# One start remainder modulo 512 bytes for all operands of TensorE in a decoder-block kernel

## The chip, the cores and the metric

The kernel runs on one core of one Trainium2 chip. The metric is the device time of one execution in microseconds (us), the median of a few runs.

## The reference

The reference is one hybrid decoder layer on a sequence of 1024 tokens of width 1024, in float32:

```python
x = x + 0.5 * gt1 * swiglu(mod(rmsnorm(x)), ffn1_w1, ffn1_w3, ffn1_w2)   # width 2816
x = x + gt2 * hybrid_mixer(mod(rmsnorm(x)), w_in, ..., w_out)            # below
x = x + 0.5 * gt3 * swiglu(mod(rmsnorm(x)), ffn2_w1, ffn2_w3, ffn2_w2)
return modulate(rmsnorm(x, g_final), shf, scf)
```

The shifts, scales and gates come from a conditioning vector through a matrix of 1024 x 11264. The mixer projects to q, k, v and three gates; 4 heads are causal differential attention (two softmax maps each, with rotary embedding), 8 channel groups a gated convolution over 3 tokens; both are normalised, joined and projected back.

## The kernel before

Everything is held transposed: features in the 128 partitions, tokens along a partition, in halves of 512. Each float32 operand of a large product is split into a high and a low part (names that end in h and l: `Wh`, `Wl`), and each product of 128 x 128 by 128 x 512 is three matmuls into one PSUM bank: high by high, high by low, low by high. In every one the first operand (128 columns, 512 bytes of a partition) is loaded into the array as weights, the stationary operand, and the second (512 columns, 2048 bytes) streams through it, the moving operand. `mm` (line 1532) and `mm_open` (line 1536) issue them; `nc.tensor.transpose` at lines 1970 and 1890 turns attention's tiles.

The two feed-forward blocks (0.5 * gate * SwiGLU) use one level of Strassen's scheme, 7 products in place of 8. Their stages, twice each:

- **plain group**, 192 matmuls, the first units of weights in the ordinary way (`plain_group`);
- **up**, 140 products j = 0 to 6 in turn, each of 12 matmuls (4 k steps x 3): stationary `Wh`, `Wl` (eight slots, filled by ScalarE and VectorE five products ahead), moving `Bh`/`Bl` number j, which are kept for the whole stage (`up`, matmuls at line 1536). Product 0 streams `Bh0`, and so on;
- **down**, 77 products of 12 matmuls (4 output tiles x 3): both operands are slots of `Wh` and `Wl` (`down_tile`, line 1536).

Between them lies the mixer, with matmuls from line 1532: projections with stationary `Mh`/`Ml` and moving `Hh`/`Hl` (24 matmuls a job, 8 k steps x 3), the output projection with moving `Gh`/`Gl` and others, and a stage that makes V in which `Hh`/`Hl` are stationary and `Mh`/`Ml` moving. Attention interleaves projections for the next head with small float32 matmuls, each recorded twice.

All tiles are placed by hand in a partition. `place` (lines 152 to 160) puts a tile at a given byte offset; the first free byte is 16512, which is 128 more than a multiple of 512. Two groups of places follow from it:

```python
base = at[0]                      # 16512: remainder 128 modulo 512
x_at = base + 88 * K + 64         # remainder 192; K is 1024
slot_at, raw_at, t_at, z_at, tmp_at = (x_at + n * K for n in (32, 64, 80, 96, 108))
```

At remainder 128 lie `Bh`/`Bl` 0, 1, 2, 3 and 5 (from `base`), `Mh`, the weights' sums `Sums`, `QK[:, 0]`, and `G2[:, 0]`. At remainder 192 lie `Wh`, `Wl`, `Raw`, `T`, `X`, `Ada`, the temporaries, `Bh`/`Bl` 4, 6 and `B12` (in places of X and others), and, because of the 8 spare elements in `QK`, also `O`, `Hh`, `Hl`, `Ml`, `Wo`, `V`, `Gh`, `Gl`. `QK[:, 1]` and `G2[:, 1]` lie at 160. Slices of an operand along k or along its 128 columns step by multiples of 512 bytes, so a tile's remainder is that of all its slices of 128 or 512 columns.

The order of the work is written out by hand; each engine runs its own list and waits on semaphores. SP and POOL issue the loads, the spills to DRAM and their reloads, each released by the engines' counts.

Of the kernel before, what the change touches and what calls it, by code (L numbers as in the profile page):

```python
# [6 lines left out]
F32R = mybir.dt.float32r  # L7
# [4 lines left out]
P = 128  # L12
D = 1024
S = 1024
# [136 lines left out]
def program(nc, up_w, down_w, units, ada, x_t, cols_d, lam_d, rope_d, square_d, out_t):  # L151
    ctx = ExitStack()
    with ctx:
# [3 lines left out]
        def place(name, shape, dtype=F32, like=None):  # L157

            size = 4
            for n in shape[1:]:  # L160
                size *= n
            offset = at[0] if like is None else like
            if like is None:
                at[0] += (size + 31) // 32 * 32
            return nc.alloc_sbuf_tensor_at(name, shape, dtype, offset=offset), offset

        K = 1024
        base = at[0]
        x_at = base + 88 * K + 64
        slot_at, raw_at, t_at, z_at, tmp_at = (x_at + n * K for n in (32, 64, 80, 96, 108))  # L170
        at[0] = tmp_at + 8 * K

        X, _ = place("X", [P, NH, KT, HALF], like=x_at)
# [10 lines left out]
        Sums, _ = place("Sums", [P, 4, HALF], like=base + 80 * K)  # L184
        Wh, _ = place("Wh", [P, SLOTS, HALF], F32R, like=slot_at)
        Wl, _ = place("Wl", [P, SLOTS, HALF], F32R, like=slot_at + 16 * K)
        Raw, _ = place("Raw", [P, 4, 2, HALF], like=raw_at)
        T, _ = place("T", [P, 8, HALF], like=t_at)
        Ada, _ = place("Ada", [P, 2, D], like=z_at)
        AdaSum, _ = place("AdaSum", [P, D], like=z_at + 8 * K)  # L190
        W2s, _ = place("W2s", [P, 4, HALF], like=tmp_at)
# [3 lines left out]
        RawB, _ = place("RawB", [P, 8, HALF], like=raw_at)  # L195

        AdaFirst, _ = place("AdaFirst", [P, KT, D], like=base)
        AdaSecond, _ = place("AdaSecond", [P, KT, D], like=base + 32 * K)
        AdaSum0, _ = place("AdaSum0", [P, D], like=t_at)
        AdaRow, _ = place("AdaRow", [P, D], like=t_at + 4 * K)  # L200
        Lam4, _ = place("Lam4", [P, 4, DH], like=t_at + 8 * K)
        LamP, _ = place("LamP", [P, 2, DH], like=t_at + 9 * K)


        Mh, _ = place("Mh", [P, RING, S], F32R, like=base)
        qk_at = base + 12 * K
        QK, _ = place("QK", [P, 2, S + 8], like=qk_at)
        CU, _ = place("CU", [P, S + 2], like=qk_at)
        CT, _ = place("CT", [P, S], like=qk_at + 4 * (S + 8))
        o_at = qk_at + 8 * (S + 8)  # L210
        O, _ = place("O", [P, QB, P], like=o_at)
        Mr, _ = place("Mr", [P, RING, S], like=o_at + 4 * K)
        h0_at = o_at + 16 * K
# [3 lines left out]
        Ml, _ = place("Ml", [P, RING, S], F32R, like=h0_at + 32 * K)  # L217

        Wo, _ = place("Wo", [P, 2, 2, S], F32R, like=h0_at)
        Rope, _ = place("Rope", [P, 2, S], like=h0_at + 44 * K)  # L220
        assert h0_at + 52 * K == x_at
        V, _ = place("V", [P, QB, HEADS * P], like=raw_at)
        Gh, _ = place("Gh", [P, GF, S], F32R, like=t_at)
        Gl, _ = place("Gl", [P, GF, S], F32R, like=t_at + 8 * K)
        NextQ, _ = place("NextQ", [P, S], like=t_at + 4 * K)
        NextK, _ = place("NextK", [P, S], like=t_at + 12 * K)

        G2, _ = place("G2", [P, 2, S + 8], F32R, like=qk_at)
        PR, _ = place("PR", [P, 3, S], like=z_at)
        SqSum, _ = place("SqSum", [P, NH, HALF], like=z_at)  # L230
        Sq, _ = place("Sq", [P, 2, HALF], like=z_at + 4 * K)
        Spread, _ = place("Spread", [P, NH, HALF], like=z_at + 8 * K)
        TmpA, _ = place("TmpA", [P, 2, HALF], like=tmp_at)
        TmpG, _ = place("TmpG", [P, 2, HALF], like=tmp_at + 4 * K)
        DT, _ = place("DT", [P, S], like=tmp_at + 4 * K)
        Out, _ = place("Out", [P, NH, KT, HALF], like=h0_at)

        Square, _ = place("Square", [P, 2, P])
        Cols, _ = place("Cols", [P, NCOLS])
        Mod, _ = place("Mod", [P, SECTIONS * KT])  # L240
        Scale, _ = place("Scale", [P, 4, KT])
        Gate, _ = place("Gate", [P, 3, KT])
        CAct, _ = place("CAct", [P, KT])
        Ones, _ = place("Ones", [P, 1])
        Mean, _ = place("Mean", [P, 1])
        MeanG, _ = place("MeanG", [P, 2])
        EpsC, _ = place("EpsC", [P, 2])
        Root, _ = place("Root", [P, 8])
        Inv, _ = place("Inv", [P, 8])
        LamS, _ = place("LamS", [P, 8])  # L250
        SubG, _ = place("SubG", [P, 1])
        NMax, _ = place("NMax", [P, 2])
        Sum, _ = place("Sum", [P, 2])
        RSum, _ = place("RSum", [P, QB, 2])
        Ratio, _ = place("Ratio", [P, 1])
        Junk, _ = place("Junk", [P, P])
        SqO, _ = place("SqO", [P, QB])
        assert at[0] <= nc.sbuf_usable_end

# [1826 lines left out]
```

## Time and profile before

| what | value |
|---|---|
| median of 3 runs | 1899.19 us (1899.11 to 1899.46) |
| profiled execution, its own time | 1899.21 us |
| its span, first to last instruction | 1897.4 us |
| PE (TensorE matmul) busy | 1842.2 us, 97% of the span, 8394 matmuls |
| PEld (weight loads) busy | 1476.9 us, 78% |
| VectorE (DVE) busy | 1260.6 us, 66% |
| ScalarE (ACT) busy | 774.0 us, 41% |
| GpSimd (POOL) busy | 273.6 us, 14% |
| DMA | 269.77 MB, mean 142 GB/s |

Times inside the span count from its start. Matmuls are pipelined: the next one starts before the recorded end of the last (each is shown as about 0.39 us long, and starts follow one another every 0.23 us), so the distance between starts is what a matmul costs, and the duration printed is not. The stages by the chain of waits: feed-forward 1 with its plain group to about 103 us, up to 497 us, down to 704 us; the mixer to about 1226 us; feed-forward 2 with its plain group to 1281 us, up to 1670 us, down to the end.

### The profile page before, as it was taken

The page shows a single profiled execution, that of the slowest core. Times are in us where ns is not written, and L with a number is a line of the kernel's source. Part 1 is how long each engine was busy: PE and PEld are TensorE (multiplying, and loading weights), DVE is VectorE, ACT ScalarE, POOL GpSimd, SP SyncE. Part 2 cuts the span into 40 slices and gives each one's busy share as a digit, 9 for nine tenths or more (in the row PEclk, how much of TensorE's full clock was granted, in tenths as well). Part 3 has the DMA queues.
Part 4 walks back from the last instruction along what each step waited for, and adds up shares of the span by engine and source line. Part 5 has one row for each costly group of instructions (what it writes and reads, how often), then busy time and mean ns, then how long its engine had stood idle before and what let it go on. Part 6 is the DMA issues. An engine that isn't in the chain of part 4 may idle for free.

```text
span 1897.4 us, 23217 instructions
## 1 busy us (share of the span) xinstructions
PE 1842.2 (97%) x8394; PEld 1476.9 (78%) x8394; DVE 1260.6 (66%) x1952; ACT 774.0 (41%) x1392; POOL 273.6 (14%) x411
## 2 busy tenths in 40 slices
PE   6999999999999999999999999999999999999997
PEld 3778888888788877888877777787888888878885
DVE  5887777767486776434226668787767666577767
ACT  4643333333344555111125556563333333344445
POOL 2011211211220000000303430101111111112000
PEclk9999999999999999999999999999999999999998
DMA  8165565664775312111201110325444544487432
GB/s 317 68 232 194 198 219 193 220 211 174 263 214 157 100 61 78 45 45 45 67 34 45 45 34 1 139 95 188 168 182 172 205 157 166 151 269 217 128 100 89
DMA packets 100529, 269.77 MB, mean 142 GB/s; under 512 B 13120, under 2 KB 13504, under 8 KB 100288
## 3 DMA queue, kind: packets, MB, share of 16 engines
q1 hardware_dynamic: 62608, 146.30, 22.3%
q0 software_dynamic: 34304, 117.46, 18.1%
q10 hardware_dynamic: 3504, 4.53, 1.0%
q8 instruction: 67, 1.10, 0.2%
q14 instruction: 46, 0.38, 0.1%
HBM read 209.53 MB, written 54.53 MB: 139 GB/s over the span
## 4 chain that ended last, share of the span: by engine, by line
PE 82%; DVE 8%; ACT 4%; issue 2%; DMA 1%; POOL 1%; ACTq 1%; DVEq 0%; POOLq 0%
PE PS L1536 60%; PE PS L1532 22%; ACTq L877 1%; DMA AdaFirst<-ada 1%; DMA TmpA<-TmpA 1%; DVE NMax L1447 1%; DVE X L1107 1%; PE PS L1970 1%; DVE SqSum L1312 0%; DVE Wl L1006 0%; DVE TmpA L1330 0%; DVE X L1343 0%; ACT X L676 0%; POOL TmpA L571 0%; ACT PR L899 0%
## 5 line engine op out<-in xcount | busy, mean ns | idle before, releaser
L1536 PE MATMUL PS<-Bh,Wh 128*128 128x512 f32 x1120 | 441.4, 394 | 3.8 <-ACT T L659 3.8
L1536 PE MATMUL PS<-Bl,Wh 128*128 128x512 f32 x1120 | 440.6, 393 | 0.0
L1536 PE MATMUL PS<-Bh,Wl 128*128 128x512 f32 x1120 | 439.9, 393 | 0.0
L1536 PEld LDWEIGHTS PS<-Bh,Wh 128*128 128x128 f32 x1120 | 209.7, 187 | 55.8 <-issue 3.7
L1536 PEld LDWEIGHTS PS<-Bh,Wl 128*128 128x128 f32 x1120 | 209.8, 187 | 50.1
L1536 PEld LDWEIGHTS PS<-Bl,Wh 128*128 128x128 f32 x1120 | 209.8, 187 | 48.9
L1536 PE MATMUL PS<-Wh 128*128 128x512 f32 x616 | 240.3, 390 | 3.4 <-DVE Wl L1041 1.7
L1536 PE MATMUL PS<-Wl,Wh 128*128 128x512 f32 x616 | 239.7, 389 | 0.0
L1536 PE MATMUL PS<-Wh,Wl 128*128 128x512 f32 x616 | 239.7, 389 | 0.0
L1038 DVE TENSOR_TENSOR Wl<-RawB,Wh 128x512 fp32r<-128x512 f32 x154 | 106.6, 693 | 136.4 <-ACT Wh L634 135.2
L634 ACT ACTIVATE Wh<-RawB 128x512 fp32r<-128x512 f32 x154 | 97.5, 633 | 229.9 <-PE PS L1536 229.9
L659 ACT ACTIVATE T<-PS 128x512 f32<-128x512 f32 x120 | 71.7, 598 | 257.2 <-PE PS L1536 257.2
L1006 DVE TENSOR_TENSOR Wl<-Sums,Wh 128x512 fp32r<-128x512 f32 x160 | 110.4, 690 | 89.0 <-ACT Wh L624 88.9
L1536 PEld LDWEIGHTS PS<-Wh 128*128 128x128 f32 x616 | 115.6, 188 | 28.2 <-DVE T L1072 2.5
L1006 DVE TENSOR_TENSOR Wl<-Raw,Wh 128x512 fp32r<-128x512 f32 x136 | 94.1, 696 | 62.4 <-ACT Wh L624 61.9
L1536 PEld LDWEIGHTS PS<-Wh,Wl 128*128 128x128 f32 x616 | 115.6, 188 | 24.2
L1536 PEld LDWEIGHTS PS<-Wl,Wh 128*128 128x128 f32 x616 | 115.6, 188 | 23.9
L1532 PE MATMUL PS<-Hh,Mh 128*128 128x512 f32 x320 | 131.0, 409 | 2.1 <-DVE Hl L1336 1.3
L624 ACT ACTIVATE Wh<-Sums 128x512 fp32r<-128x512 f32 x160 | 98.4, 623 | 79.6 <-DVE Sums L1024 52.5
L1532 PE MATMUL PS<-Hl,Mh 128*128 128x512 f32 x320 | 126.6, 396 | 0.0
L1532 PE MATMUL PS<-Hh,Ml 128*128 128x512 f32 x320 | 126.1, 394 | 0.0
L1062 DVE TENSOR_TENSOR T<-T,PS 128x512 f32<-128x512 f32 x120 | 82.3, 686 | 47.0 <-PE PS L1536 44.8
(195 smaller groups left out, 2894.8 us busy)
## 6 DMA issues: line engine op xcount, KB each, us to landing
Raw<-up_w SPq DMA_DIRECT2D x86, 512.0 KB, 5.1
Ada<-ada POOLq DMA_DIRECT2D x72, 512.0 KB, 4.3
g_dram<-T SPq DMA_DIRECT2D x88, 256.0 KB, 2.0
W2s<-down_w POOLq DMA_DIRECT2D x88, 256.0 KB, 4.3
s_dram<-W2s POOLq DMA_DIRECT2D x88, 256.0 KB, 2.4
GQ<-g_dram POOLq DMA_DIRECT2D x88, 256.0 KB, 3.6
RawB<-s_dram SPq DMA_DIRECT2D x88, 256.0 KB, 2.8
RawB<-down_w SPq DMA_DIRECT2D x66, 256.0 KB, 2.7
```

The lines of the kernel that those rows point to most:

```text
L624: nc.scalar.activation(Wh[:, slot, :], src, ACT.Copy).then_inc(w_hi, 1)
L634: nc.scalar.activation(Wh[:, 4 + m % 4, :], RawB[:, m % 8, :], ACT.Copy).then_inc(w_hi, 1)
L659: nc.scalar.activation(T[:, 4 * w + q, :], PS[:, x + (j == 1), :], ACT.Copy).then_inc(acopy, 1)
L877: act.dma_start(to[a:a + 32, :], TmpA[a ^ 32:(a ^ 32) + 32, slot, :]).then_inc(shifted[j % 2], 16)
L1006: nc.vector.tensor_tensor(Wl[:, slot, :], src, Wh[:, slot, :].bitcast(F32), ALU.subtract).then_inc(w_lo, 1)
L1038: nc.vector.tensor_tensor(Wl[:, 4 + m % 4, :], RawB[:, m % 8, :], Wh[:, 4 + m % 4, :].bitcast(F32), ALU.subtract).then_inc(w_lo, 1)
L1062: nc.vector.tensor_tensor(T[:, 4 * w + q, :], T[:, 4 * w + q, :], PS[:, x + (j != 4), :], ALU.add)\
L1107: nc.vector.tensor_tensor(out, left, right, ALU.subtract).then_inc(t_sum, 1)
L1447: nc.vector.tensor_reduce(NMax[:, c:c + 1], scores(c, 0, i + 1), AX.X, ALU.max, negate=True)\
L1532: return nc.tensor.matmul(out, lhs, rhs, start=first, stop=last)
L1536: return nc.tensor.matmul(out, lhs, rhs, start=first, stop=last, skip_group_check=True)
L1970: made = nc.tensor.transpose(PS[:, 4 + r, blk(b % 4)], PR[:, 2, blk(b)], ident)
```

## The change

Only places change. `x_at` moves by 960 bytes from `base + 88 * K + 64` to `base + 89 * K`, so that all tiles reckoned from it are at remainder 128. `QK` and `G2` get rows of S + 128 instead of S + 8 elements, so that their second rows, and `O` and all behind it up to X, are at remainder 128 too. `Junk`, 512 bytes that ScalarE writes and nobody reads, gets no place of its own and lies in the new spare part at the end of the second row of `QK`. No instruction, wait or DMA is added, removed or reordered.

```diff
-        x_at = base + 88 * K + 64
+        x_at = base + 89 * K
...
-        QK, _ = place("QK", [P, 2, S + 8], like=qk_at)
+        QK, _ = place("QK", [P, 2, S + P], like=qk_at)
         CU, _ = place("CU", [P, S + 2], like=qk_at)
-        CT, _ = place("CT", [P, S], like=qk_at + 4 * (S + 8))
-        o_at = qk_at + 8 * (S + 8)
+        CT, _ = place("CT", [P, S], like=qk_at + 4 * (S + P))
+        o_at = qk_at + 8 * (S + P)
...
-        G2, _ = place("G2", [P, 2, S + 8], F32R, like=qk_at)
+        G2, _ = place("G2", [P, 2, S + P], F32R, like=qk_at)
...
-        Junk, _ = place("Junk", [P, P])
+        Junk, _ = place("Junk", [P, P], like=o_at - 4 * P)
```

## Rows read from the trace of the kernel before

**Rows 1.** The page, part 1: busy time, share of the span, instructions.

```profile
PE 1842.2 (97%) x8394; PEld 1476.9 (78%) x8394; DVE 1260.6 (66%) x1952; ACT 774.0 (41%) x1392; POOL 273.6 (14%) x411
```

**Rows 2.** The page, part 4: the chain that ended last, by engine.

```profile
PE 82%; DVE 8%; ACT 4%; issue 2%; DMA 1%; POOL 1%; ACTq 1%; DVEq 0%; POOLq 0%
```

**Rows 3.** The chain's pieces: start us, length us, what, records of matmuls.

```profile
289.73 61.36 PE PS L1536 x264
...
498.74 177.79 PE PS L1536 x783
...
898.46 80.99 PE PS L1532 x348
...
1226.08 45.85 PE PS L1532 x205
```

**Rows 4.** Timeline of PE in the up stage: start us, length, instruction.

```profile
202.64 0.39 PE L1536 MATMUL PS<-Bh,Wh 128*128 128x512 f32 x1
...
205.44 0.39 PE L1536 MATMUL PS<-Bh,Wh 128*128 128x512 f32 x1
...
206.82 0.39 PE L1536 MATMUL PS<-Bh,Wh 128*128 128x512 f32 x1
...
208.18 0.39 PE L1536 MATMUL PS<-Bh,Wh 128*128 128x512 f32 x1
...
210.98 0.39 PE L1536 MATMUL PS<-Bh,Wh 128*128 128x512 f32 x1
```

**Rows 5.** Timeline of PE in the down stage.

```profile
558.71 0.39 PE L1536 MATMUL PS<-Wh 128*128 128x512 f32 x1
...
561.43 0.39 PE L1536 MATMUL PS<-Wh 128*128 128x512 f32 x1
```

**Rows 6.** Timeline of PE in a projection of the mixer.

```profile
831.64 0.39 PE L1532 MATMUL PS<-Hh,Mh 128*128 128x512 f32 x1
...
836.45 0.39 PE L1532 MATMUL PS<-Hh,Mh 128*128 128x512 f32 x1
```

**Rows 7.** Timeline of PE where V is made.

```profile
962.40 0.39 PE L1532 MATMUL PS<-Mh,Hh 128*128 128x512 f32 x1
...
977.17 0.40 PE L1532 MATMUL PS<-Mh,Hh 128*128 128x512 f32 x1
```

**Rows 8.** Timeline of PE in attention, a job with both operands in `Mh`/`Ml`.

```profile
1187.77 0.39 PE L1532 MATMUL PS<-Mh 128*128 128x512 f32 x1
...
1188.46 1.72 PE L1532 MATMUL PS<-V,DT 128*128 128x128 f32 x14
```

**Rows 9.** Waits of PE, 100 to 480 us: total us, times, longest us.

```profile
PE PS L1536 <- ACT T L659: 1.7, 1, 1.7
```

**Rows 10.** DVE by windows: window, length, busy us (instructions), clock, DMA share, GB/s.

```profile
351.00:477.00 126.00, 91.00 (x132) 1.00 0.54 190
...
1282.00:1655.00 373.00, 250.46 (x373) 1.00 0.48 172
```

**Rows 11.** The page, part 5: costly groups of DVE.

```profile
L1006 DVE TENSOR_TENSOR Wl<-Sums,Wh 128x512 fp32r<-128x512 f32 x160 | 110.4, 690 | 89.0 <-ACT Wh L624 88.9
...
L1006 DVE TENSOR_TENSOR Wl<-Raw,Wh 128x512 fp32r<-128x512 f32 x136 | 94.1, 696 | 62.4 <-ACT Wh L624 61.9
```

**Rows 12.** PE by windows around 500 us, columns as in Rows 10.

```profile
500.00:510.00 10.00, 10.00 (x46) 1.00 1.01 350
```

**Rows 13.** PE by windows where the clock falls, columns as in Rows 10.

```profile
975.00:982.00 7.00, 4.95 (x24) 0.99 0.00 0
...
981.90:988.70 6.80, 6.73 (x16) 0.50 0.00 0
988.70:995.50 6.80, 6.80 (x31) 1.00 0.00 0
1214.00:1217.40 3.40, 3.40 (x10) 0.50 0.22 78
1217.40:1220.80 3.40, 3.40 (x20) 1.00 0.41 154
```

## The prediction, written before the changed kernel was run

> **What bounds the kernel now.** I read the page first. PE is busy 97% of the span and DVE, the next, 66% [rows 1]; the chain that ended last runs through PE for 82% of its length [rows 2]. So the cost of one matmul is nearly the time of the kernel, and I went on to the distances between starts, by stage. The chain shows long unbroken pieces of PE [rows 3]: in down 783 matmuls in 177.79 us, which is 227.1 ns each, but in up 264 in 61.36 us, 232.4 ns each. Same shape, same line, same clock.
>
> The timeline of up shows where the difference sits [rows 4]. From 202.64 to 205.44 are 12 matmuls in 2.80 us, 233.3 ns each. From 205.44 to 208.18 are 12 in 2.74 us, 228.3 ns each, and the last six of them, from 206.82, take 1.36 us, 226.7 ns each. From 208.18 to 210.98 it is 233.3 again. These are products j = 3, 4, 5. The order of the code makes the assignment: 4 and 6 are the two products whose moving operand lies at remainder 192 modulo 512, as the weights `Wh` and `Wl` do; 3 and 5 (and 0, 1, 2) stream from remainder 128. The pattern comes twice in seven products all through the stage. In down, where weights and moving operand both lie at 192, 12 matmuls take 2.72 us, 226.7 ns each [rows 5]. So equal remainders go with 226.7 ns, a moving operand 64 bytes behind the weights with 233.3, and after a switch to equal remainders some six matmuls pass before the lower value is reached (2.74 - 2 x 1.36 = 0.02 us lost in those six).
>
> 512 columns at the full clock of 2.4 GHz are 213.3 ns; the two values are 13.3 and 20.0 above it. That is two and three times 6.7 ns. My reading, an inference: while one matmul streams, the next one's weights are read from the same partitions, the streams meet in one part of a 512-byte period two or three times according to their distance, and each meeting costs 6.7 ns. It would depend on the difference of the two remainders, not on 128 or 192 as such.
>
> **The change part by part.** After it every large operand is at 128: `base` is 16512 = 32 x 512 + 128, 89 K is a multiple of 512, and so are 4 (S + 128) = 4608 and 8 (S + 128) = 9216. Nothing is added to any queue. I price the matmuls stage by stage, all at 226.7 ns afterwards.
>
> Up, twice: 5 of 7 products of 140, 1200 matmuls, go from 233.3 to 226.7 ns: 7.9 us. The other 480 go from 228.3 to 226.7, since nothing switches any more: 0.8 us. That is 8.7 us a stage; the piece of 264 gives the same by another way, (61.36 - 264 x 0.2267) x 1680 / 264 = 9.6 us, which also holds the one slower start behind the small matmuls and is the upper bound. I take 17.4 us for both stages. PE waits there once, 1.7 us in 380 [rows 9], so all of it is on the path, as long as others keep up: DVE is busy 91.0 of 126 us and 250.5 of 373 us [rows 10], 72% and 67%, and would be at 74% and 69% after a stage 2.2% shorter. The floor that DVE alone sets for the first window is its 91.0 us, far under the 123 that PE will need.
>
> Down, twice: both operands at 192 now, both at 128 then: nothing, if only the difference counts. The DMA engines are full at 500 to 510 us [rows 12]; this stage is not asked to go faster, and the stage ahead of it has its loads gated by counts of PE and DVE, which all come earlier together. Bounds of what an earlier end of up could cost there: 0 to 2 us; I take 0.
>
> Plain groups: 144 of 192 matmuls stream from 128. The second group has a PE piece of 45.85 us on the chain [rows 3]: 144 x 6.6 = 0.9 us. The first stands ahead of the long pieces, where the chain is in DVE and ACT; I count 0 there, at most 0.9.
>
> Mixer. The piece from 898.46 us, which holds V and the q and k projections, has 348 matmuls in 80.99 us, 232.7 ns each [rows 3]; V alone is 63 in 14.77 us, 234.4 ns each [rows 7]. At 226.7 the piece saves 2.1 us. Projections run at 21 in 4.81 us, 229.0 ns each [rows 6], with `Mh` at 128 and the other three at 192: 576 in the convolution's stage and 192 in its output, less 60 counted already, are 708 x 2.3 = 1.6 us; the chain leaves PE now and then there, so I take 1.5. Attention and the last output projection have some 480 large matmuls more, 1.1 us, of which I take 0.8, because the small matmuls, ACT and DVE share the chain.
>
> DVE, ACT, POOL and the DMAs read and write at shifted places too. DVE's subtraction takes 690 ns with `Sums` at 128 against `Wh` at 192, and 696 ns with both at 192 [rows 11]. If remainders mattered to it, equal ones would cost 6 ns, which on the 160 operations of the first row is 1.0 us of an engine that is covered; it can go below nothing by the same amount. Value taken: 0. `Junk` in the spare part of `QK` is written by ACT alone, in order with its own other work: 0.
>
> Sum: 17.4 + 0.9 + 2.1 + 1.5 + 0.8 = 22.7 us. From the profiled execution's own 1899.21 us (span 1897.4 and 1.8 around it; the median of the runs is 1899.19, the same): 1876.5 us. I add 0.5 us for waits that come up when PE is earlier: **1877 us**.
>
> The clock puts a margin around it. It is at half, 1.2 GHz, for 6.8 us at 982 us, with 16 matmuls where the next 6.8 us hold 31, and for 3.4 us at 1214 us, 10 against 20 [rows 13]: losses of 3.3 and 1.7 us. Ahead of the first, PE is busy 4.95 of 7 us [rows 13]; as all such stretches shift by several us, each loss may go or grow: 5 us less, or 4 us more.
>
> Two rules of the Trainium skill bear on this. "SBUF — State Buffer", section "Who interferes with whom", gives TensorE two independent read ports, one for the moving operand and one for the weight load, and says that it never waits on anyone; by that rule no place of an operand matters and the change brings nothing. The trace speaks against it [rows 4, 5]. "TensorE: Matmul & The Clock Gate", section "Back-to-back issue gap", has N / 2.4 + 2.5 ns for a single gap, 215.8 ns for 512 columns; the lowest value here is 226.7 [rows 4, 5], and 11 ns on each large matmul stay by my count. By the page's figure some 7,000 matmuls would save an estimated 76 us more, which no row here supports.
>
> **The rivals.** *Slower: the remainder itself counts.* Streaming from 128 costs 233.3 ns wherever the weights are. Every long row agrees with that as well: 128 goes with 233.3, 192 with 226.7. The change then slows what is now fast. 1848 matmuls of down and about 1056 of `Bh4`, `Bh6` and `B12` would pay 6.6 ns: 19.2 us; the mixer's 1200 with a moving operand at 192 would go from 229 to 233.3: 5 us; the first sum's gains would not come. Near 1923 us. It decides at one point: what 128 against 128 takes. The only such rows are jobs of three matmuls in attention, where 1187.77 to 1188.46 is 230.0 ns each [rows 8], too short a run to settle, but under 233.3. Against it too: the projections stream from 192 and yet take 229.0, not 226.7, with only some weights at 128 [rows 6], so the weights' place does count.
>
> *No change.* The difference between 226.7 and 233.3 comes from something else that sets products 4 and 6 apart: they lie in X's place, the others lower in the partition. Then 1899 us. Against it: `Hh` and `Hl` of the first half lie low, those of the second high, and the timeline of projections has no two speeds by half.
>
> *Half the gain.* The streams keep their lag by history (six matmuls to settle [rows 4]), and with small matmuls and product changes in between many runs stay above 226.7, or a late load or DVE takes back a part: 11 us, 1888 us. Down speaks against it, as it holds 227.1 over 783 matmuls [rows 3].
>
> **How the numbers follow.** Forecast 0.79, half the gain 0.09, no change 0.05, slower 0.07. The likeliest case by itself: 1871 (both clock losses gone) to 1884 (clock 4 us worse, 3 us of new waits or of hidden mixer gains). For 8 in 10 over all cases I widen it to 1870 to 1888, the half case's value; what is left out is no change, slower, part of the half case and a little at each end. A change under 0.2%, 3.8 us, is what this measurement can't tell from none. Faster by more: 0.88; within: 0.05; slower: 0.07.
>
> **What would show it.** Right: in up every 12 matmuls take 2.72 us without the two-in-seven pattern, a piece of 264 takes 59.9 us; down stays at 227; V falls from 234 to 227 ns, projections from 229; the down stages of the two blocks begin 9 us and about 22 us earlier than now. DVE's means stay within 1%. The forecast is wrong if down rises to 233 (the remainder itself counts), if up stays at 233 (no effect of place), or if PE begins to wait in up for DVE's `Wl`.

## The result: 1.04% faster, and where the time went

| | before | changed |
|---|---|---|
| median | 1899.23 us | 1878.47 us (4 runs, 1877.34 to 1880.90) |
| ratio | 1 | 0.9896, 95% interval 0.9884 to 0.9909 |
| profiled execution, span | 1897.4 us | 1877.0 us |
| PE busy | 1842.2 us | 1820.2 us |
| DVE busy | 1260.6 us | 1260.8 us |

The forecast was 1877 us. The page of the changed kernel, part 1, answers to [rows 1], and two groups of part 5 to [rows 11]:

```profile
PE 1820.2 (97%) x8394; PEld 1479.3 (79%) x8394; DVE 1260.8 (67%) x1952; ACT 772.9 (41%) x1392; POOL 271.9 (14%) x411
...
L1006 DVE TENSOR_TENSOR Wl<-Sums,Wh 128x512 fp32r<-128x512 f32 x160 | 110.2, 689 | 82.8 <-ACT Wh L624 82.7
...
L1006 DVE TENSOR_TENSOR Wl<-Raw,Wh 128x512 fp32r<-128x512 f32 x136 | 93.9, 695 | 57.9 <-ACT Wh L624 57.7
```

The other engines did the same work in nearly the same time; only PE got clearly shorter. The pieces of the chain of the changed kernel (start, length, matmul records), to be read against [rows 3]:

```profile
286.97 60.01 PE PS L1536 x264
...
491.78 177.79 PE PS L1536 x783
...
890.52 79.19 PE PS L1532 x348
...
1214.11 45.68 PE PS L1532 x208
```

Up went from 61.36 to 60.01 us a piece of 264, down stayed at 177.79 to the last digit, and the piece with V went from 80.99 to 79.19. The timelines show it matmul by matmul. First up (the pattern of two in seven is gone: 24 matmuls from 195.47 to 200.91 take 5.44 us, 226.7 ns each), then a projection (33 in 7.48 us, 226.7 against 229.0 in [rows 6]), then V (60 in 13.60 us, 226.7 against 234.4 in [rows 7]), then the job in attention that [rows 8] show (3 in 0.68 us, 226.7 against 230.0):

```profile
195.47 0.39 PE L1536 MATMUL PS<-Bh,Wh 128*128 128x512 f32 x1
...
200.91 0.39 PE L1536 MATMUL PS<-Bh,Wh 128*128 128x512 f32 x1
...
822.13 0.39 PE L1532 MATMUL PS<-Hh,Mh 128*128 128x512 f32 x1
...
829.61 0.39 PE L1532 MATMUL PS<-Hh,Mh 128*128 128x512 f32 x1
...
953.22 0.39 PE L1532 MATMUL PS<-Mh,Hh 128*128 128x512 f32 x1
...
966.82 0.39 PE L1532 MATMUL PS<-Mh,Hh 128*128 128x512 f32 x1
...
1175.51 0.39 PE L1532 MATMUL PS<-Mh 128*128 128x512 f32 x1
...
1176.19 1.72 PE L1532 MATMUL PS<-V,DT 128*128 128x128 f32 x14
```

The clock, PE by windows, answers to [rows 13]. The half-speed stretch at 982 us is gone. One of the same length stands at 39.8 us, where the clock was full before; it covers small matmuls, and the first plain group behind it begins at 46.73 us instead of 44.20. The one at 1214 us is now at 1200:

```profile
39.80:46.60 6.80, 6.80 (x33) 0.50 0.19 68
...
970.00:985.00 15.00, 13.25 (x59) 1.00 0.00 0
1200.40:1203.80 3.40, 3.40 (x10) 0.50 0.44 159
```

From the starts of the long pieces the whole difference of the spans adds up (before, then changed). Not all of it is matmul distances: the stretches at half speed moved too, and the part on the prediction takes them apart.

| stage | before, us | changed, us | difference |
|---|---|---|---|
| to the first up, 103.37 and 104.42 | 103.37 | 104.42 | +1.05 |
| first up, to 498.74 and 491.78 | 395.37 | 387.36 | -8.01 |
| first down and projections, to 898.46 and 890.52 | 399.72 | 398.74 | -0.98 |
| the piece with V | 80.99 | 79.19 | -1.80 |
| attention and the rest of the mixer, to 1226.08 and 1214.11 | 246.63 | 244.40 | -2.23 |
| second plain group, to 1281.43 and 1269.23 | 55.35 | 55.12 | -0.23 |
| second up, to 1671.30 and 1650.84 | 389.87 | 381.61 | -8.26 |
| second down to the end | 226.1 | 226.2 | +0.1 |
| span | 1897.4 | 1877.0 | -20.4 |

### The profile page after: what moved, and what is told of

The parts are those of the page before. It is cut to its first block, busy times and chain, and to the rows that moved or that the text cites. A ratio compares the mean times of both kernels' runs of the same rounds, so it can differ in the third digit from the quotient of the medians.

```text
span 1877.0 us, 23217 instructions
## 1 busy us (share of the span) xinstructions
PE 1820.2 (97%) x8394; PEld 1479.3 (79%) x8394; DVE 1260.8 (67%) x1952; ACT 772.9 (41%) x1392; POOL 271.9 (14%) x411
## 4 chain that ended last, share of the span: by engine, by line
PE 86%; DVE 7%; ACT 3%; issue 1%; DMA 1%; POOL 1%; ACTq 1%; DVEq 0%; POOLq 0%
PE PS L1536 60%; PE PS L1532 25%; DVE NMax L1447 1%; DMA AdaFirst<-ada 1%; ACTq L877 1%; PE PS L1970 1%; DMA TmpA<-TmpA 1%; DVE X L1343 1%; DVE SqSum L1312 0%; DVE TmpA L1330 0%; DVE Ml L1246 0%; ACT PR L899 0%; DVE Wl L1041 0%; DVE Wl L1038 0%; DVE CT L1412 0%
## 5 line engine op out<-in xcount | busy, mean ns | idle before, releaser
L1536 PE MATMUL PS<-Bl,Wh 128*128 128x512 f32 x1120 | 435.8, 389 | 0.0
```

What stands on the lines that cost most here:

```text
L1536: return nc.tensor.matmul(out, lhs, rhs, start=first, stop=last, skip_group_check=True)
```

## The experiments

**What counts, the difference or the place?** A kernel of matmuls alone, 48 to a section, each section on a line of its own. The operands are float32r, the type in which TensorE takes the split operands (`F32R` in the code, printed as f32 in the rows). "Ahead" is the weights' start less the moving operand's, in bytes:

```diff
+ for i in range(N): nc.tensor.matmul(*at(192, 128, i), ...)   # weights at 192, moving at 128; 30 such lines
```

> A kernel that computes nothing of the reference: float32r matmuls of 128x128 by 128x512 alone, in sections of 48 with one line each, set apart by small float32 matmuls. In each section the weights start at one remainder modulo 512 and the moving operand at another. In 16 sections the moving operand is at 128 and the weights are ahead of it by 0, 32, ... 480 bytes; others have equal remainders at 0, 64, 192 and 320, the weights 64 ahead at 0, 192 and 320, and differences of 4, 8, 16 and 48 bytes. My theory (the difference counts; the weights' read meets the moving read two or three times in a matmul, 6.7 ns each): equal remainders 226.7 ns between starts at each of the places, 64 ahead 233.3 at each. From the load's 187 ns against 213.3 for the stream, the moving read gains some 1283 bytes on the weights' during a load and begins some 29 ahead; so three meetings, 233.3 ns, for the weights 32 to 288 bytes ahead, and two, 226.7, for 288 to 480 and for 0. First rival (the remainder itself counts): 233.3 wherever the moving operand is at 128, 226.7 at 192, whatever the weights do. Second rival (place has no effect): one value in all sections.

The last six us of some sections (line 59: equal at 128; 61, 63 and 71: weights 32, 64 and 192 ahead of it; 75: 256 ahead; 95: equal at 192; 99: 64 ahead of 0; 109: 16 ahead of 128). A row is start, length and count, and its length holds the count less one distances and 0.39 us for the last matmul:

```profile
28.04 6.06 PE L59 MATMUL PS<-M,W 128*128 128x512 f32 x26
39.96 6.23 PE L61 MATMUL PS<-M,W 128*128 128x512 f32 x26
52.04 6.23 PE L63 MATMUL PS<-M,W 128*128 128x512 f32 x26
100.37 6.11 PE L71 MATMUL PS<-M,W 128*128 128x512 f32 x26
124.29 6.06 PE L75 MATMUL PS<-M,W 128*128 128x512 f32 x26
244.20 6.05 PE L95 MATMUL PS<-M,W 128*128 128x512 f32 x26
267.92 6.23 PE L99 MATMUL PS<-M,W 128*128 128x512 f32 x26
327.85 6.29 PE L109 MATMUL PS<-M,W 128*128 128x512 f32 x27
```

So (6.06 - 0.39) / 25 = 226.8 ns at equal remainders, 128 or 192 alike, 233.6 at 32 or 64 ahead at two places, 228.8 at 192 ahead, and 226.8 again at 256 ahead. The first rival falls: 128 is not slow as such. The second falls too. But my count of two or three meetings falls with them: it asked for 226.7 from 288 to 480 bytes ahead, and the sections there took 233.3 for the most part; in these steps of 32 bytes every difference took what the same less 256 did.

**All at 192.** The same layout 64 bytes further:

```diff
-        at = [16512]
+        at = [16576]
```

> The changed kernel with every tile 64 bytes further, so that all operands start at remainder 192 instead of 128. If the difference counts: as the changed kernel, 1878 us within 0.2%, ratio to before 0.989, 226.7 ns a matmul in up and down. If the remainder itself counted with 192 the good one, the changed kernel could not have gained; a form in which 128 and 192 differ in some other way would show as more than 0.2% between this and the changed kernel.

Measured: 1878.99 us, ratio 0.9894 (0.9880 to 0.9909), the changed kernel's time.

**The first part of the change alone.**

```diff
-        x_at = base + 88 * K + 64
+        x_at = base + 89 * K          # QK, G2 and o_at as before; Junk goes to x_at - 512
```

> The first part of the change alone: x_at at remainder 128, the rows of QK and G2 as before, so that O, Hh0, Hl0, Ml and Wo stay at 192 while Wh, Wl, X, all B, Hh1, Hl1, V, Gh and Gl are at 128. My sum gives the feed-forward blocks 18.3 us (17.4 in up and 0.9 in the second plain group) and the mixer 4.4. In the mixer this kernel still mixes 128 and 192, so I expect 1899.2 - 18.3 and 0 to 2 us of the mixer's gain: 1880 us, ratio 0.990, the mixer still at 229 to 234 ns a matmul. A theory in which the gain is spread evenly over all large matmuls would give some 60% of it, 1887 us.

Measured: 1882.88 us, ratio 0.9912 (0.9896 to 0.9929). Two rows of its chain, of up and of the piece with V:

```profile
287.37 60.01 PE PS L1536 x264
...
892.44 81.04 PE PS L1532 x348
```

All of up's gain is there (the two stages take 387.33 and 381.67 us) and none of V's. The kernel took 2.9 us more than the 1880 us expected: up gave 16.2 us and not 17.4, and the mixer got nothing. The 4.4 us between the medians of this kernel and the changed one are what my sum had for the mixer, but part of that agreement is chance: by stages the places show 1.5 us ahead of the piece with V and 1.85 in it, and behind it the two profiled executions differ in their time at half speed, as shown further down.

**Is the period 512 or 256, and do 32 bytes matter?** Two kernels from the changed one:

```diff
-        x_at = base + 89 * K
+        x_at = base + 89 * K + 256    # the first; the second has + 32
```

> The changed kernel with X and all tiles reckoned from it 256 bytes further: Wh, Wl, X, V, Gh, Gl, Hh1 and Hl1 at remainder 384 modulo 512, the rest at 128, so that in up 5 of 7 products have weights and moving operand 256 bytes apart. By the period of 256 seen with matmuls alone: 226.7 ns in up all the same, and 1878.5 us, ratio 0.989, as the changed kernel. If the title's 512 bytes is the period: up back at about 233 ns and 1896 us.

> The changed kernel with X and all tiles reckoned from it only 32 bytes further: in 5 of 7 products of up and in the plain group the weights are 32 bytes ahead of the moving operand. With matmuls alone 32 ahead took 233.3 ns: then up and the second plain group lose all they gained, 18.3 us, and the mixer, whose tiles at h0_at stay equal to Mh, loses about 2 of its 4.4: 1898 us, ratio 0.9995. If only differences of 64 bytes or more count (a part of 64 bytes being one unit), 1878.5 us.

Measured: 256 bytes apart 1879.57 us, ratio 0.9898 (0.9884 to 0.9913); 32 bytes apart 1899.01 us, ratio 1.0000 (0.9990 to 1.0009). The same piece of up in the first and the second kernel:

```profile
286.41 60.01 PE PS L1536 x264
```

```profile
290.87 61.36 PE PS L1536 x264
```

256 bytes apart is as good as equal, and 32 bytes undo the gain to within 0.1%: the remainder that counts in this kernel is that of 256. Equal remainders modulo 512, as in the title, are enough but more than is needed.

**Fine steps.** 65 sections of 36, the weights 0 to 256 bytes ahead in steps of 4.

> Matmuls alone again, nothing of the reference: 65 sections of 36 float32r matmuls of 128x128 by 128x512, the moving operand at remainder 128, the weights ahead of it by 0, 4, 8, ... 256 bytes, one line for each section. The first such kernel refuted my two-or-three-meetings count: its settled values had a period of 256 bytes, with 226.7 ns at 0, 16 and 256 and 229 to 234 elsewhere. Theory now: the cost is a function of the difference modulo 256 with a narrow low place at 0 to about 16 bytes; so 226.7 ns at 0, some 231 to 233 at 4 and 8, 226.7 at 16, and from about 24 to 240 mostly 233, with a lower place at 192 (229). No value lies under 226.7. Rival: 226.7 is one step of a ladder, and some difference that the 32-byte steps missed is lower still, which would be a faster kernel.

```profile
19.42 6.06 PE L59 MATMUL PS<-M,W 128*128 128x512 f32 x26
28.54 6.21 PE L61 MATMUL PS<-M,W 128*128 128x512 f32 x26
37.78 6.17 PE L63 MATMUL PS<-M,W 128*128 128x512 f32 x26
56.31 6.22 PE L67 MATMUL PS<-M,W 128*128 128x512 f32 x26
296.83 6.29 PE L119 MATMUL PS<-M,W 128*128 128x512 f32 x27
380.58 6.25 PE L137 MATMUL PS<-M,W 128*128 128x512 f32 x25
575.33 6.06 PE L179 MATMUL PS<-M,W 128*128 128x512 f32 x26
```

These are 0, 4, 8, 16, 120, 156 and 240 bytes ahead: 226.8, 232.8, 231.2, 233.2, 226.9, 244.2 and 226.8 ns. No difference settled under 226.7, so there is no better place to find among them. The expected low place from 0 to 16 bytes isn't there: single differences far from 0 (120, 132, 240) also reach 226.7, the worst reaches 244, and 16 bytes took 226.9 in the first kernel (its line 109) and 233.2 here.

**Which reads meet, widths, bfloat16.**

```diff
+ *at(64 * (i % 2), 64 * (i % 2), i)         # line 69: own pair equal, next weights 64 off
+ *at(64 * ((i + 1) % 2), 64 * (i % 2), i)   # line 71: own pair 64 off, next weights equal
+ *at((0, 0, 64)[i % 3], 64, i)              # line 81: the projections before
+ *at(64, (0, 0, 64)[i % 3], i)              # line 83: V before
+ *at(0, 0, i, 480); *at(64, 0, i, 480)      # lines 85, 87: 480 moving columns
+ *at(0, 0, i, 256); *at(64, 0, i, 256)      # lines 109, 111: 256 moving columns
+ *bf(0, 0, i); *bf(128, 0, i)               # lines 115, 123: bfloat16
```

> Matmuls alone, nothing of the reference. (a) Which two reads meet: sections in which weights and moving operand alternate between remainders 0 and 64. If it is the moving read of one matmul with the load of the NEXT one's weights, then the section with own pairs equal and next weights 64 off is slow (about 233 ns), and the one with own pairs unequal and next weights equal is fast (about 227); if it is a matmul's own pair, the other way round. (b) The mixer's two patterns before the change, rebuilt: weights at 0, 0, 64 with moving at 64: 229 to 231 ns; weights at 64 with moving at 0, 0, 64: 234 ns. (c) Narrower moving operands, 480 to 256 columns, with the weights 0, 64 and 128 ahead: if stalls come from the overlap of the two reads, 64 ahead stays slower by some 7 ns as long as the stream is longer than the load's 187 ns, and the distance between starts falls to a floor set by the load near 190 to 200 ns for 320 and 256 columns. (d) bfloat16, where both reads take half the bytes: if the stall comes from bytes in flight the values lie nearer 216 ns and the period changes; if from instructions, the same 227 and 233.

```profile
25.38 6.19 PE L69 MATMUL PS<-M,W 128*128 128x512 f32 x26
37.42 6.23 PE L71 MATMUL PS<-M,W 128*128 128x512 f32 x26
97.54 6.12 PE L81 MATMUL PS<-M,W 128*128 128x512 f32 x26
109.52 6.26 PE L83 MATMUL PS<-M,W 128*128 128x512 f32 x26
116.43 10.65 PE L85 MATMUL PS<-M,W 128*128 128x480 f32 x48
127.73 10.62 PE L87 MATMUL PS<-M,W 128*128 128x480 f32 x48
234.06 6.00 PE L109 MATMUL PS<-M,W 128*128 128x256 f32 x48
240.71 5.90 PE L111 MATMUL PS<-M,W 128*128 128x256 f32 x48
258.25 6.21 PE L115 MATMUL PS<-Mb,Wb 128*128 128x512 bf16 x28
303.25 6.21 PE L123 MATMUL PS<-Mb,Wb 128*128 128x512 bf16 x28
```

(a) Both alternating sections are slow, 232.0 and 233.6 ns, so neither pair by itself is the answer. My reading is that both streams must keep their place from one matmul to the next; it is not shown beyond these sections and the switches in [rows 4]. (b) The two patterns of the mixer come out as in the kernel, 229.2 and 234.8. (c) This went against the expectation twice. A whole section of 480 columns takes 10.65 us at equal places and 10.62 at 64 ahead, where 7 ns a matmul would have made 0.33 us more; with 448 and 320 columns the two places also lie within 0.02 us, with 384 equal is shorter (8.58 against 8.73 us), with 256 it is longer (6.00 against 5.90). And 256 columns run at a start every 120 ns once settled, under the 187 to 192 ns that a weight load is recorded with; the floor that I expected does not exist, and the recorded length of a load is not the time that it holds anything up. (d) bfloat16 runs at (6.21 - 0.38) / 27 = 215.9 ns with the weights equal or 128 bytes ahead, and at the other eight differences too. The Trainium skill's formula for a single gap, N / 2.4 + 2.5 ns ("TensorE: Matmul & The Clock Gate", "Back-to-back issue gap"), gives 215.8 ns, and these unbroken runs agree with it. float32r pays 11 ns more at its best place.

**Amount loaded, and repeats.**

> Matmuls alone, nothing of the reference, 48 a section, float32r, 512 moving columns. (a) Weights of 96, 64 and 32 columns instead of 128, at equal remainders and 64 ahead. bfloat16 took 215.8 ns at every place, float32r 226.7 at equal remainders and 233.3 at 64 ahead. If the weight load's read delays the moving read, the excess over 213.3 falls with the columns loaded: from 13.3 towards 3 ns for 32 columns, and the 64-ahead sections lose their extra 6.7 too. Rival: the excess is a fixed price of a float32r matmul, the same with 32 columns. (b) The same weights and the same moving columns every time, at 0, 64 and 128 ahead: 226.7, 233.3, 233.3 if only the remainders count. (c) PSUM bank changed every third matmul: no change. (d) Differences 0, 16, 64, 120, 132, 240 and 256 bytes, three times over in turn. 0 took 226.7 in all sections so far, but 16 took 226.7 in one kernel and 233.3 in the next. Theory: the load and the stream settle into a pattern that repeats, equal remainders (0 and 256) always into the 226.7 one, others into either by how they start; then 0 and 256 are 226.7 three times, 64 is 233.3 three times and 16, 120, 132 and 240 vary. Rival: each difference has its own fixed value. (e) Equal remainders of 4, 8, 16 and 32: 226.7.

```profile
18.11 11.29 PE L59 MATMUL PS<-M,W 128*96 128x512 f32 x48
30.05 11.22 PE L61 MATMUL PS<-M,W 128*96 128x512 f32 x48
71.08 6.19 PE L67 MATMUL PS<-M,W 128*32 128x512 f32 x26
83.10 6.19 PE L69 MATMUL PS<-M,W 128*32 128x512 f32 x26
166.80 6.22 PE L83 MATMUL PS<-M,W 128*128 128x512 f32 x26
262.08 6.23 PE L99 MATMUL PS<-M,W 128*128 128x512 f32 x26
404.70 6.34 PE L123 MATMUL PS<-M,W 128*128 128x512 f32 x26
428.93 6.17 PE L127 MATMUL PS<-M,W 128*128 128x512 f32 x26
440.63 6.29 PE L129 MATMUL PS<-M,W 128*128 128x512 f32 x27
```

Weights of 32 columns (lines 67 and 69, 0 and 64 ahead) take 232.0 ns at either place: a quarter of the bytes loaded does not take the excess away, against my theory that the load's length of read sets it. With 96 columns (lines 59 and 61, whole sections) equal places are the slower ones, 230.0 ns settled against 228.3; with 64 columns they are the faster ones, 230.0 against 232.8. The 226.7 ns at equal places came only with weights of all 128 columns. Every difference gave the same value in all three rounds, 16 bytes ahead too (line 83, 233.2 ns; 64 ahead, line 99, 233.6), where I had expected 16, 120, 132 and 240 to vary; 120 and 132 settled at 226.7 each time, as in the fine steps, and 240 at 228.3, where the fine steps, from another place of the moving operand, gave 226.7. But each stood behind the same neighbours every time, and the two values for 16 bytes above, 226.9 and 233.2, came from the same two places, 144 and 128, behind other sections; so whether the start decides stays open. The same weights and columns every time, or another PSUM bank every third matmul, left 226.7 at equal places and 233.3 at 64 ahead. And equal is not enough, where I had expected 226.7 for all: both at 4 (line 123) takes 238.0 ns, both at 16 (line 127) 231.2, both at 32 (line 129) 226.9.

## Why the prediction was right, and where its reasons were not

*PE bounds the kernel and the distance between starts is the cost.* Shown: 22 us less of PE busy time gave 20.4 us less span.

*Up, 17.4 us.* Measured -8.01 and -8.26, 16.3 together. The term was 1.1 us too large. A piece of 264 lost 1.35 us, which is 8.6 us for 1680, and the settled matmuls are at 226.7 as counted. But the six pieces of the first up lost 7.8 us together, three of them a little less than their share, and the 21 us behind them 0.2; why was not traced. The assignment to products 4 and 6, read from the order of the code and two-in-seven in the timeline [rows 4], agrees with the kernel 32 bytes apart, where again only these two match the weights and the piece takes the same 61.36 us.

*Down, 0.* Right: 177.79 us both times.

*Plain group, 0.9.* The stage got 0.23 us shorter. Its matmuls did what was counted: the last one starts 54.55 us behind the first before and 53.44 us after, 1.1 us less. But the first product of up then waits longer for `T`, which ScalarE writes (before, then changed; the number in brackets is the wait):

```profile
1281.43 0.47 PE L1536 MATMUL PS<-Bh,Wh 128*128 128x512 f32 x1 [0.40 <-ACT T L659]
```

```profile
1269.23 0.47 PE L1536 MATMUL PS<-Bh,Wh 128*128 128x512 f32 x1 [1.29 <-ACT T L659]
```

*Mixer, 4.4.* Projections gave 0.98 us against 1.5, the piece with V 1.80 against 2.1. The rest gave 2.23 against 0.8, and that isn't the matmuls' doing. Set side by side, the time from the end of the piece with V to the second plain group follows the time that the clock stood at half speed in it, and hardly the places:

| kernel | at half speed there, us | length, us |
|---|---|---|
| before | 6.8 + 3.4 | 246.63 |
| first part of the change alone | 6.8 + 3.4 | 246.85 |
| 32 bytes apart | 3.4 + 3.4 | 246.03 |
| all at 192 | 6.8 | 245.67 |
| 256 bytes apart | 3.4 + 3.4 | 245.50 |
| changed | 3.4 | 244.40 |

Among the last three, which all have matching places, 3.4 us more at half speed go with 1.1 to 1.3 us. By that estimate the changed kernel would take some 246.8 us with the half-speed time of before, so the places gave this stage nothing that these rows can show, and at most about 0.5 us (32 bytes apart against the two others with 6.8 us). Each row is one execution.

*DVE and the others, 0.* Right: 689 and 695 ns against 690 and 696.

*0.5 us for new waits.* The wait for `T` behind the second plain group alone grew by 0.9 us.

*The total.* What the places gave by stages is 16.3 + 0.2 + 1.0 + 1.8 = 19.3 us, against the 22.7 us of the sum. The shifts of the clock, which the forecast had only in its margin, added 2.2 us of gain in attention and took 1.05 us ahead of the first up. So the mechanism and the large term were right, the small terms gave 3.0 us where the sum had 5.3, and that the forecast lies only 1.5 us from the measured median is in part luck. The same shows in the signs: the down stages begin 7.0 and 20.5 us earlier, not 9 and 22.

*The mechanism.* The part on which the sum rested, that the place of one operand against the other counts and that equal remainders reach 226.7 ns at 128 as at 192, is shown: by all at 192, by the 32 and 256 byte kernels, and by matmuls alone. The explanation that I put under it, two or three meetings of 6.7 ns within 512 bytes, is refuted by the period of 256, by the fine steps, and by the narrow weights and moving operands. The rule of the Trainium skill's "Who interferes with whom" ("SBUF — State Buffer"), that TensorE's two read ports are independent and it waits on nobody, agrees with the bfloat16 sections here (215.8 ns at ten places) and not with float32r, whose rate changes with the place of the weights alone (226.7 to 233.3 ns). It could as well be something other than ports: what stalls was not seen, only when.

Open: what the chip does in the 11 to 28 ns above bfloat16's 215.8, why it repeats every 256 bytes, why 16 bytes ahead settled in two ways at the same places, and why equal places are no better with other widths. No run tells these apart.

## What to carry to other kernels

Where a float32r kernel is bound by TensorE and its matmuls are 128x128 by 128x512, start the stationary and the moving operands of all of them at one multiple of 32 bytes modulo 256, and keep it from one matmul to the next; here that was worth up to 3% of each matmul affected and 1.04% of the kernel, for 448 bytes more of each partition. For narrower weights or moving operands measure first: with 96 columns of weights, and with 256 moving columns, equal places were the slower ones. Look for it by the distance between starts, not by the recorded length or the busy share, and compare products of one loop that differ only in their tiles. For bfloat16 ten places at this shape gave one value, so there is nothing to gain.

## What the runs showed of the hardware that was not expected

- float32r, 128x128 by 128x512 at full clock: 226.7 ns from start to start at equal multiples of 32 bytes, 233.3 in most others, 244 at the worst measured; bfloat16 215.8 at all ten places.
- With 96 columns of weights equal places took 230.0 ns and 64 bytes ahead 228.3; with 480, 448 and 320 moving columns the two took the same within 1 ns.
- In steps of 32 bytes the dependence repeats every 256 bytes of difference (0 to 480 ahead of one place, and one whole kernel), and 32 bytes are enough to lose all.
- Equal remainders of 4, 8 or 16 bytes are slow (238.0, 232.8, 231.2 ns), of 0, 32, 64, 128, 192 and 320 not.
- After a switch of place some six matmuls pass before the distance settles [rows 4].
- The recorded length of a weight load, 187 to 192 ns, does not bound the rate: 256 columns ran at a start every 120 ns.
